# Two diffusion-style transformer blocks on one core: projections and Fourier products moved between attention steps, diagonal products in place of transposes

## The chip, the core and the metric

The kernel runs on one core of a Trainium2 chip. The metric is the device time of one execution in microseconds. Five engines work side by side and meet only at semaphores: TensorE (PE in the profile, its weight loads PEld), VectorE (DVE), ScalarE (ACT), GpSimd (POOL) and SyncE (SP), whose queue issues the weight transfers.

## What is computed

512 tokens of width 1024 pass a first block of two layers and then a second block of one layer, in float32. Only two stages matter here. The first is the mixer of layer 0:

```python
def even_mixer(xn, xcn, w_in, w_out, sink, cos, sin, with_ctx_out):
    proj = xn @ w_in
    f_in = proj[..., :FOURIER_WIDTH]                # 4 heads of 128
    ...
    attn = window_attention(q, k, v, k_c, v_c, sink)
    y = jnp.concatenate([fourier_mix(f_in), attn], axis=-1) @ w_out

def fourier_mix(u):
    uh = u.astype(jnp.float32).reshape(B, N, FOURIER_HEADS, FOURIER_HEAD_DIM)
    y = jnp.fft.fftn(uh, axes=(1, 3), norm='ortho').real
```

The second is the mixer of the second block: a sparse attention of 8 heads (for each query block a compressed, a selected and a window branch, each with its own softmax and gate) beside a stick-breaking attention of 8 heads, whose weights are exp(log_sigmoid(z) + a running sum of log_sigmoid(-z)):

```python
    o_nsa = nsa_mixer(q_n, kc, vc, ksl, vsl, kwn, vwn, gts, positions, ...)
    o_sb = stick_breaking(q_s, k_s, v_s)
    x = x + jnp.concatenate([o_nsa, o_sb], axis=-1) @ w_out[l]
```

## The kernel before, in words

Activations lie transposed in SBUF (features on partitions, 512 tokens along the free side). Every large projection is done as three products on halves: `mm3` (lines 400 to 404) multiplies high by high, high by low and low by high; `act_weights` (L339) casts a block of weights (2048 columns) to its high half, `dve_units` (L351) subtracts to get the low half, and also adds up the modulation's matrix-vector products (L362, L365). The blocks come through two buffers `raw` in the order of `weight_units`. Products of the attentions and of the Fourier mixing are plain float32, which TensorE records as two matmuls each. A transpose is recorded as one.

Each engine's program is written out by hand in one order, with waits on semaphores. The first mixer runs so. `pe_fourier` takes the four Fourier heads c in turn: `pe_over_dims` (L978, 4 products of 256 columns into banks 5 and 6 of PSUM) gives cosine and sine parts, ACT and DVE copy them (L1007, L1024) into `ab`, and 8 products of 512 columns (L998) over the tokens give the head's result, which ACT and DVE split into `xh` and `xl` (L691, L694). Then `pe_first_attention` runs 16 jobs (query block i, pair of heads) as a pipeline of steps: step s has scores(s) (L582, masks L589), turn(s-1) (L649) and attend(s-2) (L684). Beside it DVE takes the maxima (L600, L602), copies half of the turned groups (L675), inverts the sums and multiplies the exponentials by them (`dve_scale`, L636, one instruction for each head), and subtracts (L694); ACT has the exponentials (L611, L614), the other half of the copies (L668) and the casts (L691). Turning a job's weights takes a bank of PSUM for each group of 512 columns; the banks are 4, 5 and 7, and group k waits until group k-3 has been copied.

The second mixer first has its projections (`pe_w_in`): queries of the sparse attention, its keys and values, the compression, then the stick-breaking queries `sq` (4 products of 512 columns, L402 to L404), keys `sk` (4 likewise, scaled into `ksbT` at L1832) and values `sv` (8 token-major products of 256 columns, scaled into `vsb` at L1757). `pe_second_attention` then runs 24 sparse jobs in the same kind of steps, with 4 heads each (for i = 0 to 3 and two key heads: the compressed branch of 31 keys, the selected and the window branch of 128(i+1) keys), and 8 heads of stick-breaking: scores (L1979), ACT's absolute values, exponential and logarithm (L1990 to L1996), DVE's sums (L2006 to L2017), PE's running sums (L2024 to L2027), ACT's exponential (L2038), and attend (L2048). The order of the stick steps on PE is scores(h), sums(h-1), attend(h-2); scores(h+1) waits for ACT's exponential of head h-1. `dve_scale` and `pe_turn` also serve the memory attention (4 jobs) that follows.

## Time and profile before

| What | Value |
|---|---|
| median of 3 runs | 2379.2 us (2374.57 to 2381.82) |
| the profiled execution, its own time | 2376.95 us |
| its span | 2374.9 us |
| TensorE busy (weight loads) | 2217.8 us, 93% (1763.5 us, 74%) |
| VectorE busy | 1099.2 us, 46% |
| ScalarE busy | 774.9 us, 33% |
| mean granted TensorE clock | 0.96 |
| the chain that ended last | PE 83%, DVE 8%, ACT 6% |

The span is that of one profiled execution; its own time adds 2 us around it. The clock is the share of full speed that TensorE was granted.

### The profile page before, as it was taken

Reading aid. Unit: us, or ns where it says so; the run is one execution under the profiler, and the core shown is the slowest. Engines: PE = TensorE matmul, PEld = TensorE weight load, DVE = VectorE, ACT = ScalarE, POOL = GpSimd, SP = SyncE. Lnnn points to the kernel's source line nnn. Section 1 sums busy time; section 2 is a strip of 40 time slices with the busy share of each in tenths; the row PEclk is TensorE's granted clock in tenths of the full one; section 3 lists DMA queues with packets and bytes.
Section 4 is the critical chain, followed back from the end, with each engine's and each line's share of the span. In section 5 each row is a group of like instructions: output and inputs, shape, how many; then the busy total and the mean of one; then the engine's idle time right before and its main releaser. Section 6 shows DMA issues by size and latency. Waiting matters only on the chain.

```text
span 2374.9 us, 25076 instructions
## 1 busy us (share of the span) xinstructions
PE 2217.8 (93%) x10572; PEld 1763.5 (74%) x10572; DVE 1099.2 (46%) x1550; ACT 774.9 (33%) x1149; POOL 87.5 (4%) x84
## 2 busy tenths in 40 slices
PE   6997889999994999999999999899988898999999
PEld 4665678888873888888888888777755576888887
DVE  3637755555528433333534333453474346443421
ACT  4314432222223322222322222323455735222211
POOL 0000000000001000000111100100000001111100
PEclk9999999999996999999999999899887998999999
DMA  7521146555530232323223223223100021323232
GB/s 261 188 88 59 58 133 197 184 195 167 192 103 18 90 106 89 102 98 96 93 92 98 95 98 100 68 90 114 39 1 1 0 72 36 107 89 106 85 98 84
DMA packets 190784, 236.59 MB, mean 100 GB/s; under 512 B 4096, under 2 KB 175392, under 8 KB 190544
## 3 DMA queue, kind: packets, MB, share of 16 engines
q1 hardware_dynamic: 189696, 230.42, 30.1%
q0 software_dynamic: 976, 4.57, 0.6%
q8 instruction: 83, 1.36, 0.2%
q14 instruction: 29, 0.24, 0.0%
HBM read 231.96 MB, written 2.10 MB: 99 GB/s over the span
## 4 chain that ended last, share of the span: by engine, by line
PE 83%; DVE 8%; ACT 6%; issue 2%; DMA 0%; POOL 0%; SPq 0%; DVEq 0%; ACTq 0%; POOLq 0%
PE ps L402 24%; PE ps L403 24%; PE ps L404 24%; ACT pr L611 2%; PE ps L998 1%; PE ps L848 1%; PE ps L468 1%; PE ps L649 1%; DVE pr L636 1%; PE ps L1979 1%; PE ps L582 1%; PE ps L684 1%; DVE wl L351 1%; PE ps L381 1%; DVE sa L1397 1%
## 5 line engine op out<-in xcount | busy, mean ns | idle before, releaser
L402 PE MATMUL ps<-xh,wh 128*128 128x512 f32 x1800 | 714.8, 397 | 48.5 <-DVE xl L694 26.5
L403 PE MATMUL ps<-xl,wh 128*128 128x512 f32 x1800 | 708.1, 393 | 0.0
L404 PE MATMUL ps<-xh,wl 128*128 128x512 f32 x1800 | 707.3, 393 | 0.0
L351 DVE TENSOR_TENSOR wl<-raw,wh 128x2048 fp32r<-128x2048 f32 (+1 forms) x170 | 379.0, 2230 | 493.8 <-ACT wh L339 493.8
L402 PEld LDWEIGHTS ps<-xh,wh 128*128 128x128 f32 x1800 | 341.9, 190 | 128.6 <-issue 25.8
L339 ACT CAST wh<-raw 128x2048 fp32r<-128x2048 f32 (+1 forms) x170 | 314.5, 1850 | 340.7 <-PE ps L404 263.1
L404 PEld LDWEIGHTS ps<-xh,wl 128*128 128x128 f32 x1800 | 341.7, 190 | 73.1
L403 PEld LDWEIGHTS ps<-xl,wh 128*128 128x128 f32 x1800 | 342.1, 190 | 72.0 <-issue 1.2
L402 PE MATMUL ps<-hh,wh 128*128 128x512 f32 x704 | 274.1, 389 | 0.0
L404 PE MATMUL ps<-hh,wl 128*128 128x512 f32 x704 | 273.9, 389 | 0.0
L403 PE MATMUL ps<-hl,wh 128*128 128x512 f32 x704 | 273.9, 389 | 0.0
L1251 ACT CAST hh<-tmp 128x512 fp32r<-128x512 f32 x88 | 54.7, 621 | 330.8 <-DVE tmp L1299 330.8
L404 PEld LDWEIGHTS ps<-hh,wl 128*128 128x128 f32 x704 | 132.2, 188 | 27.4
L402 PEld LDWEIGHTS ps<-hh,wh 128*128 128x128 f32 x704 | 132.2, 188 | 27.4
L403 PEld LDWEIGHTS ps<-hl,wh 128*128 128x128 f32 x704 | 132.2, 188 | 27.4
L1299 DVE TENSOR_TENSOR tmp<-ps,tmp 128x512 f32<-128x512 f32 x88 | 60.8, 691 | 142.4 <-PE ps L404 139.1
L365 DVE SCALAR_TENSOR_TENSOR acc<-raw,sc,acc 128x1024 f32<-128x1024 f32 x70 | 89.8, 1283 | 42.1 <-DMA raw<-in_ada_w 40.6
L611 ACT ACTIVATE pr<-ps,sm 128x512 f32<-128x512 f32 (+5 forms) x144 | 72.7, 513 | 98.5 <-DVE sm L598 58.4
L694 DVE TENSOR_TENSOR hl<-tmp,hh 128x512 fp32r<-128x512 f32 x88 | 61.0, 693 | 60.5 <-ACT hh L1251 60.5
L1320 POOL TENSOR_TENSOR tmp<-tmp,acc 128x512 f32<-128x512 f32 x44 | 56.9, 1295 | 775.2 <-ACT tmp L1233 775.2
L1233 ACT ACTIVATE tmp<-tmp 128x512 f32<-128x512 f32 x44 | 27.8, 632 | 166.3 <-DVE tmp L1266 166.3
L649 PE MATMUL ps<-cst,pr 128*128 128x128 f32 (+1 forms) x368 | 65.7, 326 | 13.8 <-ACT pt L668 6.0
(331 smaller groups left out, 1892.4 us busy)
## 6 DMA issues: line engine op xcount, KB each, us to landing
raw<-in_ffn_w SPq DMA_DIRECT2D x52, 1024.0 KB, 5.4
raw<-in_ada_w SPq DMA_DIRECT2D x42, 1024.0 KB, 5.2
raw<-in_ffn_wg SPq DMA_DIRECT2D x22, 1024.0 KB, 5.4
raw<-in_ffn_wu SPq DMA_DIRECT2D x22, 1024.0 KB, 5.3
raw<-in_ffn_w SPq DMA_DIRECT2D x16, 896.0 KB, 4.6
raw<-in_ffn_wd SPq DMA_DIRECT2D x16, 896.0 KB, 4.7
raw<-in_w_in SPq DMA_DIRECT2D x10, 1024.0 KB, 5.2
raw<-in_ffn_wd SPq DMA_DIRECT2D x8, 1024.0 KB, 5.0
```

The source lines that it names most:

```text
L339: e.copy(wh[k % 2][:, 0:n], raw[i % 2][:, 0:n]).then_inc(*WHI.up(i))
L351: e.tensor_tensor(wl[s][:, 0:n], r[:, 0:n], wh[s][:, 0:n].bitcast(F32), ALU.subtract).then_inc(*WLO.up(i))
L365: e.scalar_tensor_tensor(out=acc[:, :], in0=w, scalar=col, in1=acc[:, :], op0=ALU.mult, op1=ALU.add).then_inc(*VA.up((i, kk), *([i, ("sum" ...
L402: e.matmul(dst, ah, bh, start=start, stop=False)
L403: e.matmul(dst, ah, bl, start=False, stop=False)
L404: return e.matmul(dst, al, bh, start=False, stop=stop)
L611: e.activation(prs[J.name][:, J.par, g, 0:J.width], ps[:, o:o + J.width], ACT.Exp, bias=m, accum_out=sm[:, J.par, 4 + g:5 + g]).then_inc(* ...
L649: m = e.transpose(bank[0:w, o:o + P], prs[J.name][:, J.par, g, col:col + w], ident)
L694: e.tensor_tensor(dst, src, high.bitcast(F32), ALU.subtract).then_inc(*VX.up(*keys))
L1251: e.copy(hidden[f][0][:, i, :], tmp[i % 2][:, :]).then_inc(*AX.up((f, i)))
L1299: e.tensor_tensor(t, pb[2 + cc], t, ALU.mult).then_inc(*VF.up(("up", f, i)))
L1320: e.tensor_tensor(t, t, rsx, ALU.mult).then_inc(*GP.up(("gate", f, i)))
```

## The change

It has five parts; some helpers moved by a few lines, so that L636, L649, L998 and L2038 of the kernel before are L632, L650, L994 and L2042 in the changed one.

1. The stick-breaking keys and values leave the projections and are done by `pe_stick_in` in 16 pieces, one in each of the first 16 steps of the sparse attention, between scores(s) and turn(s-1), in bank 7: 8 pieces of values, then 8 half products of keys. The weight blocks change places accordingly (`sv` before `sk`); four blocks are prepared (cast and subtraction) in steps 1, 5 and 9 for these and in 18 and 20 for the output projection.
2. Of the Fourier mixing, head 0 stays; the 24 products over tokens of heads 1 to 3 are done two at a time in steps 0 to 11 of the first attention, in bank 7. `ab` gets four buffers, `over_dims` four banks. Three more modulation units (13, 14, 15) are added up between the attention's steps.
3. The softmax's scaling goes into the turn: instead of multiplying each head's exponentials, DVE makes a diagonal matrix of the inverse sums for all heads of a job in one instruction, and PE multiplies by it instead of transposing.
4. The turns have banks 4 and 5 alone, so group k waits for the copy of group k-2.
5. ACT loads one table set, `natural_log_exp_and_others`, ahead of the stick-breaking heads. The sparse outputs of query blocks 0 and 1 are first copied to `tmp` and split into `xh` and `xl` in steps 17 and 19, since the pieces still read those.

```diff
+            eye = ident.unsqueeze(1).broadcast_to([P, nh, P])
+            e.tensor_tensor(diagonal(J), eye, rs.unsqueeze(2).broadcast_to([P, nh, P]), ALU.mult).then_inc(
+                *VS.up((J.name, "diagonal", J.n)))
-            for g in range(nh):
-                p = prs[J.name][:, J.par, g, 0:J.width]
-                e.tensor_scalar(p, p, rs[:, g:g + 1], None, ALU.mult).then_inc(*VS.up((J.name, "scaled", J.n, g)))
...
-                        m = e.transpose(bank[0:w, o:o + P], prs[J.name][:, J.par, g, col:col + w], ident)
+                        m = e.matmul(bank[0:w, o:o + P], prs[J.name][:, J.par, g, col:col + w], diagonal(J)[:, g],
+                                     start=True, stop=True, skip_group_check=True)
...
+        def pe_over_tokens(e, c, tb):
+            if c and tb == 0:
+                e.wait_ge(*VX["mix", c - 1])
+            e.wait_ge(*dims_copied(c, tb))
+            for z, tab in ((0, "cn"), (1, "sn")):
+                m = e.matmul(pb[7], ab[c][:, tb, z * P:(z + 1) * P], b1(tab, T, tb * T), start=tb == 0 and z == 0,
+                             stop=tb == 3 and z == 1)
...
+            for c in range(1, 4):
+                pe_over_dims(e, c)
+            for tb in range(4):
+                pe_over_tokens(e, 0, tb)
+            e.wait_ge(*dims_copied(3, 2))
+            pe_modulation(e, 0, 2, pb[0])
...
             for s in range(n + 2):
                 if s < n:
                     pe_scores(e, first_[s])
+                if s < 12:
+                    c, tb = 1 + s // 4, s % 4
+                    pe_over_tokens(e, c, tb)
+                if s == 12:
+                    e.wait_ge(*VX["mix", 3])
+                    pe_modulation(e, 0, 3)
                 if 0 < s <= n:
-                    pe_turn(e, first_[s - 1])
+                    pe_turn(e, first_[s - 1], (4, 5))
...
+                if s in (1, 4, 6, 8, 12):
+                    dve_units(e, {1: 13, 4: 14, 6: 15, 8: 16, 12: 17}[s])
...
+        def pe_stick_in(e, p):
+
+            if p < 8:
+                y, tb = p // 4, p % 4
+                u = of["sv", y]
+                if tb == 0:
+                    e.wait_ge(*WLO[u])
+                if p:
+                    e.wait_ge(*AE["sv", ((p - 1) // 4, (p - 1) % 4)])
+                pe_proj_tok(e, 7, u, 0, 256, xh, xl, tb).then_inc(*MM.up(("sv", y, tb), *([("w", u)] if tb == 3 else [])))
+                return
+            c, half = (p - 8) // 2, p % 2
...
+            for k in range(4 * half, 4 * half + 4):
+                m = mm3(e, pb[7], hi[:, k, cols], lo[:, k, cols], xh[:, k, :], xl[:, k, :], k == 0, k == NC - 1)
...
+        steps = {1: ("sv", 1), 5: ("sk", 0), 9: ("sk", 1), 18: ("out2", 0), 20: ("out2", 1)}
...
                 elif s < NN + 8:
                     pe_stick_scores(e, s - NN)
+                if s < 16:
+                    pe_stick_in(e, s)
                 if 0 < s <= NN:
-                    pe_turn(e, nsa_[s - 1])
+                    pe_turn(e, nsa_[s - 1], (4, 5))
...
                 elif s < NN + 8:
+                    if s == NN:
+                        e.preload_act_table_set("natural_log_exp_and_others")
                     act_stick_logs(e, s - NN)
...
+                if s in steps:
+                    act_weights(e, of[steps[s]])
...
+                if 8 < s < 16 and s % 2:
+                    dve_stick_in(e, "sk", (s - 9) // 2)
+                if s in steps:
+                    dve_units(e, of[steps[s]])
```

TensorE from the Fourier stage to the first scores (`fT` is the Fourier input, `ab` its parts, `b1c` the tables, `acc` the modulation's sums). Before:

```order
L978 MATMUL ps<-b1c,fab 128x256 x4
L967 MATMUL ps<-cst,tmp 128x128 x6
L978 MATMUL ps<-b1c,fab 128x256 x4
L998 MATMUL ps<-b1c,fab 128x512 x8
L978 MATMUL ps<-b1c,fab 128x256 x4
L381 MATMUL ps<-cst,acc 128x1 x8
L998 MATMUL ps<-b1c,pr 128x512 x8
L978 MATMUL ps<-b1c,fab 128x256 x4
L998 MATMUL ps<-b1c,fab 128x512 x8
L998 MATMUL ps<-b1c,pr 128x512 x8
L582 MATMUL ps<-kT,qT 128x128
```

and now:

```order
L986 MATMUL ps<-b1c,fT 128x256 x4
L968 MATMUL ps<-cst,tmp 128x128 x6
L986 MATMUL ps<-b1c,fT 128x256 x12
L994 MATMUL ps<-b1c,ab 128x512 x8
L379 MATMUL ps<-cst,acc 128x1 x8
L580 MATMUL ps<-kT,qT 128x128
...
L587 MATMUL ps<-bcs 128x128 x2
L994 MATMUL ps<-b1c,ab 128x512 x2
```

Of the 32 products over tokens, 8 stay ahead of the attention, and two follow each of twelve scores.

ScalarE over one stick-breaking head in the steady state (`C2S` holds the logarithms, `pt` the weights). Before:

```order
L1990 ACTIVATE C2S<-ps 128x512
L1992 ACTIVATE C2S<-ps 128x768
L1994 ACTIVATE C2S<-C2S 128x1280
L1996 ACT_TABLE_LOAD
L1996 ACTIVATE C2S<-C2S,cst 128x1280
L2038 ACT_TABLE_LOAD
L2038 ACTIVATE pt<-ps 128x512
L2038 ACTIVATE pt<-ps 128x768
L691 CAST xh<-ps 64x512
```

and now:

```order
L1994 ACTIVATE C2S<-ps 128x512
L1996 ACTIVATE C2S<-ps 128x768
L1998 ACTIVATE C2S<-C2S 128x1280
L2000 ACTIVATE C2S<-C2S,cst 128x1280
L2042 ACTIVATE pt<-ps 128x512
L2042 ACTIVATE pt<-ps 128x768
L692 CAST xh<-ps 64x512
```

Of 16 table loads in this stage one is left, ahead of the first head.

## Rows read from the trace of the kernel before

**Rows 1.** Windows by stage: Fourier, first attention, stick keys and values, sparse, stick.

```profile
core 0: us, PE busy (x) PEld busy (x) DVE busy (x) ACT busy (x) POOL busy (x), PEclk, DMA share, GB/s
144.14:187.54 43.40, 40.00 (x121) 20.80 (x119) 15.55 (x21) 7.96 (x16) 0.00 (x0) 0.96 0.29 96
187.54:279.65 92.11, 68.31 (x720) 53.57 (x720) 75.29 (x184) 48.34 (x148) 0.00 (x0) 0.93 0.11 36
1643.02:1689.64 46.62, 45.31 (x290) 41.19 (x289) 11.94 (x8) 11.70 (x14) 0.00 (x0) 1.00 0.29 91
1689.64:1801.65 112.01, 97.89 (x720) 64.27 (x721) 82.23 (x274) 60.92 (x229) 0.00 (x0) 0.84 0.00 1
1801.65:1902.18 100.53, 86.65 (x323) 51.66 (x321) 35.40 (x89) 70.07 (x77) 0.00 (x0) 0.88 0.00 0
```

**Rows 2.** Timeline of PE in the Fourier stage: start, duration, line, tiles, count, [idle before].

```profile
144.14 2.25 PE L978 MATMUL ps<-b1c,fab 128*128 128x256 f32 x8
...
149.22 7.03 PE L998 MATMUL ps<-b1c,fab 128*128 128x512 f32 x16
156.09 1.03 PE L978 MATMUL ps<-b1c,fab 128*128 128x256 f32 x4
...
158.95 1.96 PE L381 MATMUL ps<-cst,acc 128*128 128x1 f32 x16
```

**Rows 3.** Timeline of PE, one step of the first attention.

```profile
218.48 0.37 PE L582 MATMUL ps<-kTs,qT 64*128 64x128 f32 x1 [1.29 <-ACT pr L611]
...
220.02 1.29 PE L649 MATMUL ps<-cst,pr 128*128 128x128 f32 x10
...
223.63 0.37 PE L582 MATMUL ps<-kTs,qT 64*128 64x128 f32 x1 [1.07 <-ACT pr L611]
```

**Rows 4.** Timeline of DVE, the same step.

```profile
219.04 1.02 DVE L636 TENSOR_SCALAR pr<-pr,sm 128x640 f32<-128x640 f32 x2
...
220.60 0.82 DVE L600 TENSOR_REDUCE sm<-ps 128x1 f32<-128x640 f32 x1
```

**Rows 5.** Timeline of PE: four plain float32 products of 128 columns.

```profile
1962.02 1.05 PE L468 MATMUL ps<-cst,hs 128*128 128x128 f32 x8
```

**Rows 6.** Timeline of PE, turns of the sparse attention.

```profile
1743.04 1.54 PE L649 MATMUL ps<-cst,pr 128*128 128x128 f32 x12
...
1748.29 3.08 PE L649 MATMUL ps<-cst,pr 128*128 128x128 f32 x12 [0.59 <-DVE pr L636]
...
1780.43 0.66 PE L649 MATMUL ps<-cst,pr 128*128 128x128 f32 x4 [2.51 <-DVE pt L675]
```

**Rows 7.** Groups by line: busy, mean ns, idle before; first whole span, then the sparse stage.

```profile
L351 DVE TENSOR_TENSOR wl<-raw,wh 128x2048 fp32r<-128x2048 f32 (+1 forms) x170 | 379.0, 2230 | 493.8 <-ACT wh L339 493.8
L339 ACT CAST wh<-raw 128x2048 fp32r<-128x2048 f32 (+1 forms) x170 | 314.5, 1850 | 340.7 <-PE ps L404 263.1
...
L365 DVE SCALAR_TENSOR_TENSOR acc<-raw,sc,acc 128x1024 f32<-128x1024 f32 x70 | 89.8, 1283 | 42.1 <-DMA raw<-in_ada_w 40.6
...
L636 DVE TENSOR_SCALAR pr<-pr,sm 128x31 f32<-128x31 f32 (+4 forms) x92 | 24.1, 326 | 0.8
```

**Rows 8.** Timeline of ACT, one stick-breaking head.

```profile
1873.22 1.27 ACT L1994 ACTIVATE C2S<-C2S 128x1280 f32<-128x1280 f32 x1
1874.51 1.28 ACT L1996 ACT_TABLE_LOAD   x1
1875.80 1.36 ACT L1996 ACTIVATE C2S<-C2S,cst 128x1280 f32<-128x1280 f32 x1
1877.18 1.28 ACT L2038 ACT_TABLE_LOAD   x1
```

**Rows 9.** Timeline of PE, the same head.

```profile
1869.92 2.42 PE L1979 MATMUL ps<-qsT,ksbT 64*128 64x512 f32 x8 [1.24 <-ACT pt L2038]
...
1876.22 2.38 PE L2048 MATMUL ps<-pt,vsb 128*128 128x512 f32 x8
1879.83 2.42 PE L1979 MATMUL ps<-qsT,ksbT 64*128 64x512 f32 x8 [1.24 <-ACT pt L2038]
```

More of the change, by code:

```diff
@@ L222, in program @@
         part.close()
+        first.close()
         part = ExitStack()
+        pt = sb("pt", [P, 2, 1280], F32, part)
+        ab = [sb(f"ab{c}", [P, 4, 256], F32, part) for c in range(4)]
         b1c = sb("b1c", [P, NB1C], F32, part)
-        fab = sb("fab", [P, 3072], F32, part)
-        fT = fab[:, 0:2048].rearrange("p (c t) -> p c t", c=4)
+        fT = sb("fT", [P, 4, T], F32, part)
         qT = sb("qT", [P, 4, T], F32, part)
@@ L266, in program @@
         hid = sb("hid", [P, 2, 2 * NCMP], F32, second)
+        rcol = sb("rcol", [P, 4], F32, second)
+        rsm = ssum
         part = ExitStack()
@@ L1011, in act_fourier @@
             act_values(e, "v", pb[2], T, vt)
[L1012 to L1017 removed]
+            act_values(e, "vc", pb[3], LC, vct)
+            for c in range(1, 4):
+                act_over_dims(e, c)
+            act_fourier_put(e, 0)
         def dve_over_dims(e, c):
@@ L1665, in pe_w_in @@
[L1665 to L1676 removed]
+            for y in range(2):
+                u = of["sq", y]
+                e.wait_ge(*WLO[u])
+                for cc in range(2):
+                    c = 2 * y + cc
+                    e.wait_ge(*(VE["scaled", "gates"], AE["kc"], VE["sq", 0], VE["sq", 1])[c])
+                    pe_proj(e, cc, u, cc * P, xh, xl).then_inc(*MM.up(("in2", "sq", c), *([("w", u)] if cc else [])))
+                    if c == 0:
+                        pe_rope2(e, "kw", "ks", kwT[:, 0, :])
+                        for b in range(4):
+                            m = e.transpose(pb[2][:, b * 24:(b + 1) * 24], tmp[1][0:24, b * P:(b + 1) * P], cst[0:24, 0:24])
+                        m.then_inc(*ST.up(("turned", "gates")))
+                        pe_head_sums(e, "kc", "kw", 0, n)
+                    elif c == 1:
+                        pe_head(e, "kc", None, 3, 0, n)
+                    elif c == 2:
+                        pe_cmp_turn(e, 1)
+                        for j in range(2):
+                            pe_rope2(e, ("kc", j), ("kc", 0) if j else "kw", kcC[:, j * NCMP:(j + 1) * NCMP], NCMP, "kc")
+                if y == 0:
+                    pe_cmp(e, 1, 1)
+                else:
+                    e.wait_ge(*AE["hid", 1])
+                    e.wait_ge(*VE["sq", 3])
+                    for j in range(2):
+                        for f in range(2):
+                            m = e.matmul(pb[1][0:NCMP, j * P:(j + 1) * P], hid[:, f, j * NCMP:(j + 1) * NCMP],
+                                         w2c[:, 1, f, :], start=f == 0, stop=f == 1)
+                    m.then_inc(*MM.up(("in2", "vc")))
@@ L1971, in pe_stick_scores @@
                 e.wait_ge(*EX["nsa", NN - 1, 3])
+                e.wait_ge(*VE["sk", 3])
             elif h == 1:
@@ L2095, in act_second_attention @@
                             r, cs, cols, src = nsa_places(J, o)
-                            act_put(e, xh[r, cs, cols], src, ("nsa", J.n, o))
+                            if J.i > 1:
+                                act_put(e, xh[r, cs, cols], src, ("nsa", J.n, o))
+                            else:
+                                e.copy(nsa_early(J.i)[r, cs], src).then_inc(*AE.up(("nsa", J.n, o)))
+                    if s in (17, 19):
+                        i = (s - 17) // 2
+                        e.wait_ge(*AE["nsa", 6 * i + 5, 1])
+                        act_put(e, xh[:, 0:4, i * P:(i + 1) * P], nsa_early(i), ("early", i))
                 elif s > 1:
```

216 lines of the change are left out of this document (75 added, 141 removed).

## The prediction

> **What bounds the kernel now.** I read the page first: TensorE is busy 93% of the span and carries 83% of the chain, so a stage gets shorter either where TensorE has less to do or where it now waits. Then I cut the two mixers into stages with the windows [rows 1]. Nearly all of the change lies in five of them, from 144.14 to 279.65 us (Fourier stage and first attention) and from 1643.02 to 1902.18 us (stick keys and values, sparse attention, stick-breaking). In the Fourier stage PE is busy 40.0 of 43.4 us, and with the keys and values 45.3 of 46.6: there the work itself sets the time. In the three attention stages it is not so plain: PE is busy 68.3 of 92.1 us at a granted clock of 0.93, 97.9 of 112.0 at 0.84 and 86.7 of 100.5 at 0.88. A busy figure taken at half clock is inflated, so I multiply: at full clock (2.4 GHz) the work is about 68.3 x 0.93 = 64, 97.9 x 0.84 = 82 and 86.7 x 0.88 = 76 us. The room that work from elsewhere can fill is the rest, 28, 30 and 24 us. What ends PE's waits there is to be seen in single steps. In the first attention scores(s+1) waits 1.1 to 1.3 us for ACT's exponentials [rows 3], and those wait for DVE, which goes round once in 5.15 us, 1.02 of it in the two scalings and 0.82 in one maximum [rows 4]. In the stick stage ACT is the pacemaker: one head takes 9.91 us, PE is idle for 1.24 of it until ACT's last exponential [rows 9], and between ACT's instructions stand two table loads of 1.28 us [rows 8].
>
> **Price of a turn.** The trace has no product with a diagonal, but plain float32 products of the same 128 columns: four of them, eight records, last 1.05 us [rows 5]. A burst's last record has a tail of 0.16 us that does not hold up what follows (16 records last 7.03 us and the next begins after 6.87 [rows 2]), so one product costs (1.05 - 0.16) / 4 = 0.22 us. A transpose costs 1.54 / 12 = 0.13, or 0.12 without the tail [rows 6]. Each of the 368 turned blocks thus costs TensorE 0.10 us more: 144 in the first attention, +14; 192 in the sparse one, +19; 32 in the memory attention, +3. As bounds I take 0.05 and 0.14 (the tail left in). The Trainium skill speaks against this part: its page TensorE: Matmul & The Clock Gate (Terms) says that transpose mode makes FP32 four times faster. By that a product would cost 0.50 us and the 336 blocks of the two mixers would add over 120 us; rows 5 and 6 give a factor of 1.8, and I go by them. For DVE the scaling becomes one instruction of 256 or 512 columns. I take 0.42 and 0.69 us, by proportion from the 0.82 us that DVE takes over 640 columns and what it pays per instruction; a fused 0.27 is the low end, 1.02, that is no gain, the high one [rows 4]. That frees DVE of some 0.6 us a step, 9 in the first attention and 8 of the 24 us in the sparse one [rows 7].
>
> **First mixer.** Eight products over tokens take 6.87 us [rows 2], 0.86 each. Now 24 of the 32 leave the Fourier stage. What stays is: 16 products over dimensions at 0.43 (two of them, four records, take 1.03 less the tail; the eight of 144.14, with a wait in them, 2.25) 7, six transposes 1, 8 products over tokens 7, the modulation 2, waits for copies 1.5 [rows 2]. That is 18.5 us in place of 43.4: **-25**. In the attention they come back. A step at 640 columns had 5.15 - 1.07 = 4.1 us of PE work [rows 3]; it gets 1.72 (two products) and ten turned blocks at 0.10, and is 6.8 us long. DVE's round is then about 4.5 us, hidden in it. The whole stage: 64 + 20.6 + 14 = 99 us of PE work at full clock, and PE no longer waits in the first twelve steps except some 0.5 us in every second one, where the third group waits for its bank (two banks in place of three). The last steps keep the waits that they had. Three added modulation units are 6 x 1.28 us of DVE [rows 7], hidden as long as PE's step is 2 us longer than DVE's round; uncovered they would cost 8. I take 101 us in place of 92.1: **+9**, between +5 and +16. Net **-16**.
>
> **Keys and values.** The 46.6 us of PE work go from before the sparse attention into its steps: -46.6 there. The attention then has 82 + 46.6 + 19 = 148 us of PE work, in 16 steps of some 6.2 us and 8 of some 5.5. With that much work between scores(s) and scores(s+1), DVE and ACT (82 and 61 us busy in all) are always ahead in the first 16 steps, so TensorE should stay at full clock there, where it had 0.84 [rows 1]. What is not hidden: the blocks of weights prepared in steps 1, 5 and 9 (cast 1.85 after the copies on ACT, subtraction 2.23 on DVE [rows 7]) delay the next maxima by about 1 us beyond PE's step, 3 in all; those of steps 18 and 20, where no piece gives cover, by 1 to 3 each, 4 in all. And from step 16 on a turn of three or four groups on two banks waits for copies that stand behind the maxima and exponentials of the next job; with three banks such a wait took 2.51 us [rows 6]. It comes earlier now and is partly repaid by the shorter scaling: +1 on each of four turns, 4. Sum 148 + 11 = 159, against 46.6 + 112.0 = 158.6: **0**. Half clock in the last eight steps would add to it, a better fit would take from it: -10 to +15. This is the step that I am least sure of.
>
> **Stick-breaking.** 15 of 16 table loads go, 19.2 us of ACT [rows 8]. But per head only PE's wait can be saved, 1.24 of the 9.91 us: PE has 8.67 us of work per head [rows 9], and ACT's round without the loads (9.91 - 2.57 = 7.34) is below it. Over eight heads 10 us. The rest of the gain is at the ends, where nothing overlaps: the first head, during which PE waits for the turns' copies behind the logarithm, and the last head's chain through logarithm, sums and exponential, three loads or 4 us; and the stretches at half clock, which followed from waits. I take 84 us in place of 100.5: **-16**, between -10 (the waits alone) and -24 (all loads and full clock). The Trainium skill's ScalarE: Activation LUTs (What ACT_TABLE_LOAD costs) adds a drain of 1.38 us to each load. By it a head would save 5.3 us of ACT's time; the logarithm starts 0.01 us after the load's end and the load 0.02 after the exponential's [rows 8], so there is no such drain here, and PE's work caps the gain in either case.
>
> **The rest.** Memory attention: eight turned blocks a step on PE +0.8, DVE's scaling -0.45, four steps: +1 (-2 to +3). The early copies and late splits of the sparse outputs cost nothing: ACT has 51 us idle in that stage [rows 1]; without that cover 1 us each. Sum -16 + 0 - 16 + 1 = -31 against the profiled execution's 2376.95: **2346 us**. The median of the runs shown is 2.2 us above that execution, so I say 2347.
>
> **Rivals.** (a) *The moved work is hidden whole.* Then the first mixer saves 25, the keys and values 46.6 and the stick stage 20: 2377 - 91 = 2286. Against it: TensorE's room at full clock in the two receiving stages is 28 and 30 us, and the turns alone take 14 and 19 of it. Chance 0.03. (b) *The stick stage gains little*, since TensorE sets its pace and remains at half clock at its ends: -6 in place of -16, and the sparse stage loses 5: 2361. Chance 0.15. (c) *Slower: the sparse steps become a chain of turn, copy, turn on two banks, at half clock.* Place: steps 12 to 24. Price: at half clock the twelve transposes took 3.08 in place of 1.54 us [rows 6]. If the clock of the sparse stage stays at the old 0.84, 148 us of work take 148 / 0.84 = 176, and with the 11 of waits 187: +28; with the bank waits at 2.5 us in each of the eight long turns another 12, and the first attention at 0.93 +7. That gives 2346 + 47 = 2393. It decides from a clock of about 0.87 in the sparse stage with such waits. For it: half clock came in this stage whenever PE waited. Against: the pieces fill just these waits. Chance 0.06. (d) *Better fit:* TensorE at full clock throughout and almost no waits in the sparse stage, -9 there, -18 first mixer, -20 stick: 2331. Chance 0.2. (e) That the moved work stands where it is hidden from nobody (a piece waits for its weight block, a transfer being late) would show as waits of PE on the subtraction; the blocks have landed long before (the DMA share is 0.00 in the sparse stage [rows 1]), 0.02, at some 2370.
>
> **How the numbers follow.** My forecast, 2347, has 0.54. The range 2329 to 2366 takes in (b) and (d), leaves out (a), (c), (e) and the ends of my own terms where several coincide. A measurement of this kernel can tell some 0.3%, 7 us, from no change. Faster by more needs under 2372: my case, (a), (b), (d), 0.90 after the tails; within it 0.05; slower 0.05.
>
> **What the changed profile would show.** Right: the Fourier stage under 21 us, the first attention near 101 with a clock near 1; the sparse stage from the last `sq` product to the first stick scores near 159 us with waits of PE for ACT and DVE only behind the prepared blocks and from step 16 on; L650 at 0.22 us a block; one table load in the stick stage, heads 8.7 us apart there, with no wait on L2042. Wrong: a turned block at 0.4 us or more at full clock; steps without pieces as long as those with; stick heads still 9.9 us apart.

## The result, and the profile after

The changed kernel took **2365.8 us** (median of six, 2360.3 to 2370.4), the kernel before beside it 2378.2 (2374.6 to 2381.8): a ratio of 0.9948, 95% interval 0.9931 to 0.9965. It is faster, by 12.4 us where 31 were forecast: 0.5%, with the interval clear of 1. The time lies 19 us above the forecast of 2347, just under the range's upper end of 2366. The execution that was profiled is the slowest of the six, 2370.41 us, 6.5 us less than the profiled one of before. All stage figures below are from profiled executions.

First the windows by stage of the changed kernel, with the columns of [rows 1]: Fourier stage, first attention, sparse attention with the keys and values in it, stick-breaking.

```profile
144.84:161.58 16.74, 16.28 (x73) 11.51 (x71) 6.73 (x12) 6.62 (x13) 0.00 (x0) 1.00 0.19 63
161.58:280.22 118.64, 105.58 (x912) 80.49 (x912) 76.90 (x177) 51.42 (x150) 0.00 (x0) 0.94 0.16 54
1643.40:1809.63 166.23, 156.59 (x1186) 125.67 (x1184) 85.95 (x206) 76.82 (x246) 0.00 (x0) 0.94 0.10 33
1809.63:1896.50 86.87, 80.21 (x340) 50.12 (x339) 35.01 (x88) 49.67 (x61) 0.00 (x0) 0.96 0.00 1
```

| stage | before [rows 1] | after | difference | forecast |
|---|---|---|---|---|
| Fourier | 43.4 | 16.7 | -26.7 | -25 |
| first attention | 92.1 | 118.6 | **+26.5** | +9 |
| keys, values and sparse attention | 158.6 | 166.2 | **+7.6** | 0 |
| stick-breaking (up to the next projection) | 100.5 | 86.4 | -14.1 | -16 |
| sum | | | -6.7 | -32 |

The two profiled executions differ by 6.5 us, so nothing is left for the rest of the kernel. (The next projection begins at 1895.99; the last window runs half a microsecond on.) The two receiving stages took back more than the Fourier stage gave, and the gain that remains is the stick-breaking's. The places to look at are the 17.5 us too much in the first attention and the 7.6 in the sparse one.

**One step of the first attention that goes wrong.** The timeline of PE in the changed kernel, two steps, a normal one and a long one. L994 is the piece over tokens, L650 the turn by diagonals, L685 the product with the values.

```profile
201.44 1.94 PE L994 MATMUL ps<-b1c,ab 128*128 128x512 f32 x4
203.22 2.55 PE L650 MATMUL ps<-tmp,pr 128*128 128x128 f32 x20
205.70 0.88 PE L685 MATMUL ps<-pt,vt 128*64 128x128 f32 x12
...
208.48 1.94 PE L994 MATMUL ps<-b1c,ab 128*128 128x512 f32 x4
210.25 1.95 PE L650 MATMUL ps<-tmp,pr 128*128 128x128 f32 x16
214.31 1.22 PE L650 MATMUL ps<-tmp,pr 128*128 128x128 f32 x4 [2.11 <-ACT pt L669]
215.46 1.55 PE L685 MATMUL ps<-pt,vt 128*64 128x128 f32 x12
...
219.33 1.94 PE L994 MATMUL ps<-b1c,ab 128*128 128x512 f32 x4
```

From piece to piece it is 7.04 us in the first and 10.85 in the second. In the second PE does eight of its ten turned blocks and then stands for 2.11 us before the third group, which needs the bank of the first group back: ACT's copy (L669) has not come. What follows the wait is at half clock besides: four records take 1.22 us, and twelve of L685 1.55, where twelve took 0.88 a step before. The same stretch on DVE and on ACT shows why the copy is late. L363 is the modulation unit, L598 the maxima, L600 their scaling, L609 the exponentials.

```profile
207.35 0.61 DVE L695 TENSOR_TENSOR xl<-ps,xh 64x128 fp32r<-64x128 f32 x2 [0.39 <-ACT xh L692]
207.99 2.60 DVE L363 SCALAR_TENSOR_TENSOR acc<-raw,sc,acc 128x1024 f32<-128x1024 f32 x2
210.62 0.82 DVE L598 TENSOR_REDUCE sm<-ps 128x1 f32<-128x640 f32 x1
```

```profile
211.73 0.80 ACT L609 ACTIVATE pr<-ps,sm 128x640 f32<-128x640 f32 x1 [4.13 <-DVE sm L600]
...
213.68 0.57 ACT L669 COPY pt<-ps 128x512 f32<-128x512 f32 x1
```

The scores have left PE by 208.5 (the piece behind them begins at 208.48). DVE is in a unit of 2.60 us until 210.59, so the maximum begins 2 us late; ACT idles 4.13 us for it, and only behind its two exponentials, at 213.68, does it copy the bank that PE was done with at about 211.3. The three longest steps (10.59, 10.85 and 9.25 us from piece to piece, beginning at 190.85, 208.48 and 226.36) are just those behind the units of steps 4, 6 and 8. The unit of step 1 makes no long step: the turns near it have eight blocks, two groups for two banks, and no third group that waits.

**Sparse attention.** The timeline of PE in its late steps, where no piece is left.

```profile
1776.58 2.00 PE L650 MATMUL ps<-tmp,pr 128*128 128x128 f32 x16
1781.50 3.44 PE L650 MATMUL ps<-tmp,pr 128*128 128x128 f32 x16 [2.92 <-DVE pt L676]
...
1786.34 2.03 PE L650 MATMUL ps<-tmp,pr 128*128 128x128 f32 x16
1790.72 3.31 PE L650 MATMUL ps<-tmp,pr 128*128 128x128 f32 x16 [2.35 <-DVE pt L676]
```

Four groups on two banks: two groups, a wait of 2.9 or 2.4 us for a copy, two more groups, and these at half clock (16 records 3.4 us in place of 2.0).

**Stick-breaking.** One head on ACT after, against [rows 8]: no load is left between exponential (L1998), logarithm (L2000) and the last exponential (L2042), and ACT now has idle time before it.

```profile
1854.10 1.27 ACT L1998 ACTIVATE C2S<-C2S 128x1280 f32<-128x1280 f32 x1
1855.40 1.36 ACT L2000 ACTIVATE C2S<-C2S,cst 128x1280 f32<-128x1280 f32 x1
1857.30 1.30 ACT L2042 ACTIVATE pt<-ps 128x512 f32<-128x512 f32 x2 [0.53 <-PE ps L2031]
```

PE goes from head to head without a wait, 1850.80 and 1859.40 in the next rows, 8.60 us against 9.91 in [rows 9].

```profile
1850.80 2.42 PE L1983 MATMUL ps<-qsT,ksbT 64*128 64x512 f32 x8
...
1859.40 2.42 PE L1983 MATMUL ps<-qsT,ksbT 64*128 64x512 f32 x8
```

### The profile page after: what moved, and what is told of

Its sections match the earlier page's. It is cut to its first block, busy times and chain, and to the rows that moved or that the text cites. A ratio compares the mean times of both kernels' runs of the same rounds, so it can differ in the third digit from the quotient of the medians.

```text
span 2368.6 us, 25694 instructions
## 1 busy us (share of the span) xinstructions
PE 2238.4 (95%) x10940; PEld 1801.6 (76%) x10940; DVE 1079.3 (46%) x1444; ACT 759.4 (32%) x1136; POOL 87.6 (4%) x84
## 4 chain that ended last, share of the span: by engine, by line
PE 87%; DVE 7%; ACT 4%; issue 1%; DMA 0%; SPq 0%; DVEq 0%; ACTq 0%
PE ps L400 24%; PE ps L402 24%; PE ps L401 24%; PE ps L650 3%; PE ps L580 2%; PE ps L685 2%; PE ps L849 1%; PE ps L466 1%; ACT pr L609 1%; PE ps L994 1%; DVE wl L349 1%; ACT wh L337 1%; PE ps L1983 1%; PE ps L2028 1%; PE ps L379 1%
## 5 line engine op out<-in xcount | busy, mean ns | idle before, releaser
L402 PEld LDWEIGHTS ps<-hh,wl 128*128 128x128 f32 x704 | 132.2, 188 | 27.5
L400 PEld LDWEIGHTS ps<-hh,wh 128*128 128x128 f32 x704 | 132.2, 188 | 27.4
L401 PEld LDWEIGHTS ps<-hl,wh 128*128 128x128 f32 x704 | 132.2, 188 | 27.3
L650 PE MATMUL ps<-tmp,pr 128*128 128x128 f32 (+1 forms) x736 | 99.8, 289 | 20.0 <-ACT pt L669 10.3
L650 PEld LDWEIGHTS ps<-tmp,pr 128*128 128x128 f32 (+1 forms) x736 | 92.4, 195 | 31.9 <-ACT pt L669 11.7
L363 DVE SCALAR_TENSOR_TENSOR acc<-raw,sc,acc 128x1024 f32<-128x1024 f32 x70 | 89.8, 1283 | 43.5 <-DMA raw<-in_ada_w 41.9
L609 ACT ACTIVATE pr<-ps,sm 128x512 f32<-128x512 f32 (+5 forms) x144 | 72.7, 514 | 96.8 <-DVE sm L596 51.2
```

The costliest lines, as they stand in the source:

```text
L363: e.scalar_tensor_tensor(out=acc[:, :], in0=w, scalar=col, in1=acc[:, :], op0=ALU.mult, op1=ALU.add).then_inc(*VA.up((i, kk), *([i, ("sum" ...
L400: e.matmul(dst, ah, bh, start=start, stop=False)
L401: e.matmul(dst, ah, bl, start=False, stop=False)
L402: return e.matmul(dst, al, bh, start=False, stop=stop)
L609: e.activation(prs[J.name][:, J.par, g, 0:J.width], ps[:, o:o + J.width], ACT.Exp, bias=m, accum_out=sm[:, J.par, 4 + g:5 + g]).then_inc(* ...
L650: m = e.matmul(bank[0:w, o:o + P], prs[J.name][:, J.par, g, col:col + w], diagonal(J)[:, g], start=True, stop=True, skip_group_check=True)
```

## The experiments

Each was timed in five rounds against the kernel before on the same chip. The ratios are to that kernel, whose median was 2376 to 2378 us in every batch, so they can be set beside the change's own 0.9948; differences between medians of two batches can be off by those 2 us. The theory: modulation units that clump on DVE, copies that stand behind exponentials on ACT, and two banks instead of three, together make PE wait; not the work that was moved. The rival: TensorE's added work sets both stages.

### First four: units, pieces, rows, table

**e1, units spread.** One of a unit's two instructions at the end of a step, where two stood together.

```diff
-                if s in (1, 4, 6, 8, 12):
-                    dve_units(e, {1: 13, 4: 14, 6: 15, 8: 16, 12: 17}[s])
+                halves_ = {1: (13, 0), 2: (13, 1), 3: (14, 0), 4: (14, 1), 5: (15, 0), 6: (15, 1), 7: (16, 0), 8: (16, 1), 12: (17, 0), 13: (17, 1)}
+                if s in halves_:
+                    dve_half_unit(e, *halves_[s])
```

> The changed kernel, with each modulation unit of the first attention (two DVE instructions of 1.30 us in a row at the end of steps 1, 4, 6, 8, 12) dealt out one instruction a step, at the ends of steps 1 to 8, 12 and 13. Theory T (the units in DVE's order delay the maxima, the exponentials and so the copy of the first turned bank, and TensorE stands before the third bank): the three long steps of 10.6, 10.85 and 9.25 us fall to about 7.1 to 7.6, the attention goes from 118.6 to 109 to 112 us, the run from 2366 to 2357 to 2360. Rival R (TensorE's added work and its clock set the stage): the attention stays within 2 us of 118.6 and the run at 2364 to 2367.

Measured: **2355.7 us, 0.9914 (0.9900 to 0.9929)**. The attention took 110.48 us, in the window of that run:

```profile
162.33:272.81 110.48, 102.48 (x913) 78.27 (x913) 76.93 (x177) 51.03 (x150) 0.00 (x0) 0.97 0.18 58
```

8.2 us less, with the same number of products and DVE instructions. PE is idle 8.0 in place of 13.1 us and busy 3.1 less. Its work at full clock is 102.48 x 0.97 = 99.4 us, the changed kernel's (105.58 x 0.94 = 99.2) within the rounding of the clock, so the 3.1 are half clock.

The idle part is the sure one. Two runs below have the changed kernel's first attention untouched: it took 116.43 us in e11 and 119.63 in e5. PE was idle in them for 13.9 and 13.4 us, as in the changed kernel, but busy for 102.5 and 106.3.

```profile
161.69:278.12 116.43, 102.50 (x913) 78.84 (x913) 76.93 (x177) 51.37 (x150) 0.00 (x0) 0.97 0.17 55
```

With e9, which repeats this run's edit (110.77 us, 8.8 idle), spreading the units takes 4 to 6 us off the idle time in every pair. How much half clock stands behind the waits differs by up to 3.8 us between executions of the same code, and e11 has no more of it than e1. The step that took 10.85 us now takes 7.94. PE, the same two pieces and what lies between:

```profile
206.55 1.94 PE L1012 MATMUL ps<-b1c,ab 128*128 128x512 f32 x4
208.33 1.95 PE L668 MATMUL ps<-tmp,pr 128*128 128x128 f32 x16
211.06 0.71 PE L668 MATMUL ps<-tmp,pr 128*128 128x128 f32 x4 [0.79 <-ACT pt L687]
...
214.49 1.94 PE L1012 MATMUL ps<-b1c,ab 128*128 128x512 f32 x4
```

The wait is 0.79 us, not 2.11, and what follows is at full clock. So the clump is one cause, worth 6 to 9 us of the stage and 8 to 10 of the whole time (by ratio and by median); the expected "about 7.1 to 7.6" for the long steps was a little too good.

**e2, all Fourier pieces ahead**, the pieces of each quarter in banks 7 and 4 in turn.

```diff
-            for tb in range(4):
-                pe_over_tokens(e, 0, tb)
-            e.wait_ge(*dims_copied(3, 2))
-            pe_modulation(e, 0, 2, pb[0])
+            for c in range(4):
+                for tb in range(4):
+                    pe_over_tokens(e, c, tb)
+                if c == 0:
+                    e.wait_ge(*dims_copied(3, 2))
+                    pe_modulation(e, 0, 2, pb[0])
...
-                if s < 12:
-                    c, tb = 1 + s // 4, s % 4
-                    pe_over_tokens(e, c, tb)
```

> The changed kernel, with all sixteen Fourier pieces over tokens done before the first attention (two banks in turn), the units, the two turn banks and the diagonals as in the changed kernel. The Fourier stage grows by 12 pieces of 1.73 us, from 16.7 to 37 to 40 us. Theory T (the long steps come from DVE's order, not from the pieces): they stay long, the attention falls by the pieces' 20.6 us alone, to 98, and the run is within 3 us of 2366. Rival A (the pieces fill time in which TensorE would wait): the attention falls only to 102 to 108, the run rises to 2370 to 2376. Rival B (the pieces are what pushes the steps over): the attention falls to 90 to 94 and the run to 2358 to 2362.

Measured: **2380.7 us, 1.0018 (1.0009 to 1.0027)**: rival A, and past its upper end. Its Fourier stage and its attention:

```profile
144.91:181.82 36.91, 36.91 (x120) 20.44 (x119) 8.11 (x14) 6.51 (x14) 0.00 (x0) 1.00 0.09 29
181.82:295.94 114.12, 87.14 (x866) 73.50 (x865) 75.32 (x175) 51.18 (x149) 0.00 (x0) 0.93 0.17 56
```

That was the most telling run. With 20 us of pieces taken out of it, the attention is only 4.5 us shorter than the changed kernel's 118.6 (2.3 than e11's), and 22 us longer than the 92.1 of before. Here my theory was wrong too: it had taken the waits for fixed. PE waited 13.7 us for ACT's copies, against 6.3 with the pieces. So the pieces do hide waits, some 16 us of them (20.6 less 4.5), but for the most part waits that the change itself had made: with three banks, in e8, 16.7 us of the stage go.

**e3, rows scaled and transposed again** in all three attentions, the rest as changed.

```diff
-            eye = ident.unsqueeze(1).broadcast_to([P, nh, P])
-            e.tensor_tensor(diagonal(J), eye, rs.unsqueeze(2).broadcast_to([P, nh, P]), ALU.mult).then_inc(
-                *VS.up((J.name, "diagonal", J.n)))
+            for g in range(nh):
+                p = prs[J.name][:, J.par, g, 0:J.width]
+                e.tensor_scalar(p, p, rs[:, g:g + 1], None, ALU.mult).then_inc(*VS.up((J.name, "scaled", J.n, g)))
```

> The changed kernel, with the rows scaled by DVE and turned by transposes again in all three attentions, the rest as changed. Theory T: TensorE has 0.1 us less for each turned block, DVE 0.7 to 1.3 us more a step, in front of units and maxima: the long steps grow to 11 to 12 us, the others shorten by at most 1 us, and the run is at 2363 to 2370. Rival R (TensorE's added work sets the stage): the attention falls by most of the 14 us that the products by the diagonals add there, to 105 to 108, and the run to 2350 to 2356.

Measured: **2352.1 us, 0.9900 (0.9884 to 0.9915)**, 14 us under the changed kernel. The number is the rival's, the place is not: the first attention fell by 3.1 us only, the sparse part from 166.2 to 151.0.

```profile
160.24:275.78 115.54, 94.43 (x769) 66.14 (x769) 85.17 (x193) 50.62 (x150) 0.00 (x0) 0.90 0.17 56
1639.27:1790.23 150.96, 134.68 (x1010) 100.56 (x1008) 93.86 (x277) 77.11 (x246) 0.00 (x0) 0.94 0.11 36
```

In the first attention the theory comes nearer: the long steps stay at 11.05, 10.65 and 10.69 us from piece to piece, the normal ones fall from 7.0 to 6.3, and PE's waits for ACT's copies grow from 6.3 to 11.0 us. In the sparse one PE is busy 22 us less (156.6 to 134.7), and 15 of them come off the stage (against e11's 162.0 it is 11): there TensorE's work is what counts. The first attention has modulation units in its steps and the sparse one none; that this is the reason for the difference was not tested.

**e4, the kernel before with the table load alone.**

```diff
                 elif s < NN + 8:
+                    if s == NN:
+                        e.preload_act_table_set("natural_log_exp_and_others")
                     act_stick_logs(e, s - NN)
```

> The kernel before, with one load of the table that holds both Exp and Ln ahead of the stick heads and nothing else. If the changed kernel's gain in the stick stage (100.5 to 86.4 us) is this load alone, the heads stand 8.5 to 8.7 us apart, the stage falls by 10 to 13 us and the run is at 2365 to 2368, as fast as the whole change. If the gain came from the smaller DVE and PE work around it, the heads stay 9.5 us or more apart and the run is at 2373 to 2378.

Measured: **2362.2 us, 0.9940 (0.9927 to 0.9954)**, 14.0 us faster with this one line, 3 us beyond the expected range. It is as fast as the whole change. The heads stand 8.60 us apart, and the stick stage fell by 16.0 us:

```profile
1800.93:1885.48 84.55, 80.04 (x323) 48.85 (x321) 35.57 (x89) 49.87 (x61) 0.00 (x0) 0.93 0.00 1
```

### Four more: banks, and the diagonals by themselves

**e5, the third bank back in the sparse attention from job 16 on** (the last key piece has then left bank 7).

```diff
+        switch = nsa_[16].k0
+
+        def late_banks(k, before_=False):
+            def at_(k):
+                return (4, 5)[k % 2] if k < switch else (7, 4, 5)[(k - switch) % 3]
...
-                    pe_turn(e, nsa_[s - 1], (4, 5))
+                    pe_turn(e, nsa_[s - 1], late_banks)
```

> The changed kernel, with bank 7 given back to the sparse attention's turned blocks as soon as the last key piece has left it (from job 16 on, three banks in turn). Its PE rows there show waits of 0.88, 2.92, 2.35 and 0.98 us for a copy out of one of two banks. Theory B (two banks cost the late steps): they go, the sparse steps end 4 to 7 us earlier, the run is at 2359 to 2362. Rival (the same steps wait next for their maxima or for the weight units behind steps 18 and 20): at most 1.5 us, 2364 to 2366.

Measured: **2356.4 us, 0.9919 (0.9907 to 0.9931)**, 9.4 us under the changed kernel, more than theory B gave. The same turns as above, now PE's L655:

```profile
1776.82 1.82 PE L655 MATMUL ps<-tmp,pr 128*128 128x128 f32 x8 [2.02 <-DVE pt L682]
...
1781.01 5.22 PE L655 MATMUL ps<-tmp,pr 128*128 128x128 f32 x32
```

Four groups (32 records) follow each other without a wait. The part up to the stick scores took 157.5 us, and the stick stage gained too: PE waits 2.4 us in it for the last copies in place of 4.4, and its granted clock is 1.00 in place of 0.96. e9, with the same edit, has the same two stages within 0.02 us (157.54 and 81.36).

```profile
1643.07:1800.59 157.52, 153.06 (x1186) 122.50 (x1184) 85.96 (x206) 76.95 (x246) 0.00 (x0) 0.96 0.11 35
1800.59:1881.95 81.36, 76.76 (x338) 48.06 (x337) 34.94 (x88) 49.20 (x61) 0.00 (x0) 1.00 0.00 1
```

**e6, e1 and e3 together.**

> The changed kernel with both edits of the first four runs that gained: modulation units one instruction a step, and rows scaled by DVE with transposes. If the two prices are independent (10 us and 14 us below the changed kernel): 2340 to 2344. If DVE, which with the rows is 8 us busier in the first attention, has no room left for a spread unit, the halves give only 3 to 6 us: 2346 to 2350.

Measured: **2346.9 us, 0.9881 (0.9865 to 0.9898)**, inside the second case: from e3, spread units gave 5 us, not 10. With rows PE waits 7.4 us for ACT's copies again, against 2.6 with diagonals: DVE has less room for the half unit.

**e7, the kernel before with the diagonals alone** (the edit of e3 the other way round, on three banks).

> The kernel before, with the diagonal products alone in all three attentions, on its three banks. If their price is TensorE's time whatever stands around them, the first attention goes from 92 to 100 us or more, the sparse attention from 112 to about 125, the run to 2388 to 2396. If their price needs the two banks and the pieces of the changed kernel, both stages grow by at most 3 us and the run is at 2374 to 2382.

Measured: **2375.3 us, 0.9989 (0.9978 to 0.9999)**. They cost nothing there: the attention took 91.98 us and the sparse attention 112.07, within 0.2 us what they take in [rows 1].

```profile
188.86:280.84 91.98, 81.96 (x865) 70.67 (x865) 67.76 (x168) 48.79 (x148) 0.00 (x0) 0.94 0.11 36
1691.15:1803.22 112.07, 108.72 (x896) 80.90 (x897) 74.59 (x203) 61.57 (x229) 0.00 (x0) 0.92 0.01 1
```

PE is 13.7 and 10.8 us busier, all of it in time in which it had waited. Once the pieces stand between the steps, the same exchange costs 9 to 14 us (e1 to e6 8.8, e9 to e10 9.7, change to e3 13.7).

**e8, e2 with three banks in the first attention.** Modulation 3's products go behind the last turned block of step 12.

```diff
-                if s == 12:
-                    e.wait_ge(*VX["mix", 3])
-                    pe_modulation(e, 0, 3)
...
-                    pe_turn(e, first_[s - 1], (4, 5))
+                    pe_turn(e, first_[s - 1])
...
+                if s == 12:
+                    J = first_[s - 1]
+                    k = max(k for k, _ in score_groups(J) if k % 3 == 2)
+                    e.wait_ge(*turned(J, k))
+                    pe_modulation(e, 0, 3)
```

> The run with all Fourier pieces ahead of the attention (2380.7 us, attention 114.1, long steps 10.9, 10.7, 10.7), with three banks for the turned blocks of the first attention. Theory (a late exponential costs through the copy of the bank that the third group waits for): the long steps fall to 8 to 9, the attention to 104 to 108, the run to 2371 to 2375. Rival (the late maxima delay the step by themselves, whatever the banks): the attention stays at 111 or more and the run at 2377 to 2381.

Measured: **2366.3 us, 0.9952 (0.9936 to 0.9968)**, 14.4 us under e2. The attention fell by 16.7 us, more than I had expected.

```profile
182.29:279.66 97.37, 82.12 (x866) 70.22 (x865) 75.16 (x175) 50.13 (x149) 0.00 (x0) 0.95 0.20 66
```

The waits of PE in that stage, first in e2 with two banks, then in e8 with three (us in total, times, longest):

```profile
PE ps L650 <- ACT pt L669: 13.7, 4, 4.3
PE ps L580 <- ACT pr L609: 9.3, 5, 3.7
PE ps L650 <- DVE pt L676: 2.4, 3, 0.8
```

```profile
PE ps L580 <- ACT pr L609: 13.7, 8, 3.7
```

With three banks all waits for copies are gone, and those for exponentials (L609) grow a little. The units clump in both.

### Combinations, and whether the pieces pay

**e9, e1 and e5 together; e10, e1, e3 and e5 together.**

> The changed kernel with its own diagonals, with the modulation units one instruction a step and the third bank given back from sparse job 16 on. The two gains lie in different stages (10 us and 10 us alone): if they add, 2344 to 2348. If one takes the other's time away (later waits, another stretch at half clock), 2350 or more.

> As the run before it, with rows scaled by DVE and transposes in place of the diagonals. With the pieces beside them both stages are near TensorE's own time, so the 0.1 us for each turned block should still count: 2335 to 2341. If with three late banks and spread units TensorE has slack again, as it had in the kernel before, where the diagonals cost nothing: 2342 to 2347.

Measured: e9 **2348.9 us, 0.9873 (0.9856 to 0.9890)**, a little short of full addition; e10 **2339.2 us, 0.9836 (0.9815 to 0.9857)**, 9.7 us under it and 39 under the kernel before: the fastest version of the study. The rows won in both stages (110.8 to 107.1 us and 157.5 to 150.8).

**e11, the changed kernel without its table load** (the diff of e4, taken out).

> The changed kernel without its one load of the table that holds Exp and Ln. If the load is all that the change gains (it took 14 us off the kernel before, alone), this run is as slow as the kernel before: 2377 to 2381. If half of the stick stage's gain comes from the rest of the change: 2370 to 2374.

Measured: **2377.7 us, 1.0002 (0.9989 to 1.0016)**. Its stick stage took 99.1 us and ACT shows the loads again:

```profile
1862.36 1.27 ACT L1998 ACTIVATE C2S<-C2S 128x1280 f32<-128x1280 f32 x1
1863.65 1.28 ACT L2000 ACT_TABLE_LOAD   x1
1864.94 1.36 ACT L2000 ACTIVATE C2S<-C2S,cst 128x1280 f32<-128x1280 f32 x1
```

Together with e4 this closes the account: one load is all that the change gains. Its three large parts come to nothing together, within the 4 us that the interval leaves.

**e12 to e15, Fourier pieces ahead with spread units:** e13 is e8 with e1's edit, e14 that with rows, e12 that with the late bank too, e15 is e12 again. In these four the products of modulation 3 stand before the last turned block of step 12, which writes over their bank, so that modulation is not the reference's; the work is the same.

> As the run with rows, halves and the late bank, but with all Fourier pieces ahead of the first attention, which then has three banks. With clumped units and diagonals the Fourier stage and the attention took 134.3 us this way and 135.4 as changed. If moving the pieces is worth what hides beside them once units no longer clump, this run is 3 to 8 us slower than the one with the pieces between the steps: 2341 to 2348. If three banks give as much as the moved pieces, it is within 2 us of it.

> The changed kernel with all Fourier pieces ahead of the first attention, three banks there, and the modulation units one instruction a step. Against the run with spread units and the pieces between the steps (16.7 and 110.5 us of the two stages, 2355.7 in all). If the move pays by what hides beside it, this one has 36.9 us and 95 to 98, 5 to 8 us more in the first mixer: 2361 to 2364. If the third bank gives back as much as the move, 36.9 and 88 to 91: 2354 to 2358.

> The same with rows scaled by DVE and transposes, against the run with rows and spread units (16.7 and 109.1, 2346.9 in all). If the move pays, 36.9 and 96 to 99, 2353 to 2358; if not, 2345 to 2348.

> The run with all Fourier pieces ahead, rows, spread units and the late third bank, once more: 2345 to 2352 if its first measurement (2349.6) holds.

Measured: e12 2349.6 us (0.9881, 0.9863 to 0.9900), e15 2348.9 (0.9882, 0.9868 to 0.9895), e13 2363.1 (0.9941, 0.9928 to 0.9953), e14 2355.7 (0.9916, 0.9903 to 0.9930). All four are on the side of "the move pays"; e12 lies 1.6 us above even the range that it had given for that, so the move was worth some 10 us there and not 3 to 8.

**e16 and e17: e13 and e12 with those products behind the block**, as in e8.

> The changed kernel with all Fourier pieces ahead of the first attention, three banks there, the modulation units one instruction a step, and the products of modulation 3 at the end of step 12. If the move pays by what hides beside it once units are spread: 36.9 us and 95 to 98 for the two stages (16.7 and 110.5 with the pieces between the steps), 2360 to 2364 in all. If not: 2354 to 2358.

> The same with rows scaled by DVE, transposes, and the late third bank, against the run with the pieces between the steps (16.7 and 107.1, 2339.2 in all). If the move pays: 2346 to 2351. If not: 2337 to 2341.

Measured: e16 **2361.4 us, 0.9933 (0.9919 to 0.9948)**; e17 **2351.0 us, 0.9879 (0.9859 to 0.9899)**. The first attention of e16 and of e17:

```profile
182.46:278.53 96.07, 81.86 (x866) 70.10 (x865) 75.17 (x175) 49.98 (x149) 0.00 (x0) 0.95 0.21 67
```

```profile
181.63:280.14 98.51, 69.75 (x722) 55.07 (x721) 83.01 (x191) 49.71 (x149) 0.00 (x0) 0.90 0.20 65
```

**The first mixer, all runs** (Fourier stage plus first attention, us):

| pieces, banks | clumped units | spread units |
|---|---|---|
| before (rows, three banks, two units in the steps) | 135.5 | |
| the same with diagonals | e7 135.4 | |
| ahead, two banks, diagonals | e2 151.0 | |
| ahead, three banks, diagonals | e8 134.3 | e16 133.0, e13 132.2 |
| between the steps, two banks, diagonals | change 135.4, e11 133.2, e5 136.4 | e1 127.2, e9 127.5 |
| ahead, three banks, rows | | e17 135.4 |
| between the steps, two banks, rows | e3 132.3 | e6 125.8, e10 123.9 |

Each figure is one profiled execution, and the same code differs by up to 3 us (change, e11, e5). Read down the first column: giving up the bank costs 16.7 us, moving the pieces gives back 15.6 (14.6 to 17.8 with e5 and e11). Read down the second: with spread units the move with its lost bank gains 5.8 us with diagonals (e16 to e1: 5.7 us of the whole time) and 11.5 with rows (e17 to e10: 11.8). Spreading the units gains 8.2 with two banks and the pieces between the steps, 1.3 with three banks and the pieces ahead, which is no more than executions differ. Bank and place of the pieces change together in these two figures; two banks with the pieces ahead and spread units was not run. The waits speak for the bank: a third one takes all of PE's waits for copies away with the units still in clumps (e2 to e8), and spread units take 6.3 us of them down to 2.6 with two banks (e1). So the units and the lost bank are in the main one price, not two: a third bank lets PE finish its turn while an exponential is late, two do not.

## Why the prediction was right or wrong

- **Price of a turn: right.** Eight products took 1.95 us and ten 2.55, which is 0.22 and 0.24 each without the tail of 0.16; DVE's diagonal is 0.42 us at 256 columns, the value taken, and 0.69 at 512. The Trainium skill's factor of four (TensorE: Matmul & The Clock Gate, Terms), 0.50 us by my estimate from it, is not seen here: against the 0.12 us of a transpose the factor is 1.8 to 2.
- **Fourier stage, -25: right** (-26.7; the waits for copies that I had allowed for did not come).
- **First attention, +9: wrong, +26.5, and this is the step that failed.** The work was right: 99 us at full clock forecast, 99.2 measured. What failed is the sentence that "PE no longer waits in the first twelve steps except some 0.5 us in every second one", and the one that the three added units are "hidden as long as PE's step is 2 us longer than DVE's round; uncovered they would cost 8". They were not hidden: a unit is 2.60 us in one piece, DVE's order puts it ahead of the next maxima, and a mean slack of 2.3 us a step (6.8 less 4.5) does not cover 2.60 at once. I counted DVE's time where its order decides. That e1 gains 8.2 us in this stage, so near my 8, is luck: my 8 was the time of six DVE instructions, and what was measured is PE's idle time and half clock behind five units, 6 to 9 us by the executions of the same code. In the sum, the 17.5 us too much are 11 us of idle time (13.1 where I had 2) and 6.4 of half clock (105.6 less 99.2), which I had put at nothing by taking 99 us of work as 99 us of time. I priced the bank at 0.5 us; a late exponential makes it 2.11 and half clock behind it (e2 against e8: 16.7 for the whole stage without pieces). Last, my sum had 2 us for all waits though I had written that "the last steps keep the waits that they had"; in e1, 3.7 of the 8.0 us of idle time are one wait for an exponential at the end. The range for this term, +5 to +16, did not hold it; e1 would be +18.4, so the clump alone does not bring the stage back to the forecast either.
- **Keys and values, 0: too good, by 7.6 us in the profiled run.** The work was right again: 148 forecast, 156.59 x 0.94 = 147.2. The same code took 162.0 and 160.4 us in e11 and e16, 163.2 and 163.5 in e1 and e8, 160.3 in e2, so some 4 us of the 7.6 belong to this one execution; it is the slowest of six. What stays is the bank again, "+1 on each of four turns, 4": with the third bank given back 157.5, 4.4 us less than the mean of those five, and 5 more in the stick stage (86.4 to 81.4), which I had not connected with it at all. With rows in place of diagonals the stick stage keeps its 86.4 us in spite of the third bank (e10); why is open. Keys and values were the step that I had named as the least sure.
- **Stick-breaking, -16: right in size and cause.** -14.1; e4 has -16.0 in this stage and -14.0 us of the whole time by the load alone, e11 +11.9 by taking it out. The head is 8.60 us apart (8.67 forecast) and no drain beyond the loads' 1.28 us appears, as said ahead of the result.
- **Memory attention and the rest, +1: near enough.** From its first scores to the projection behind it the memory attention took 22.7 us before and 22.8 after (1975.70 to 1998.37, 1969.22 to 1991.98), and the four stages sum to -6.7 of -6.5.
- **The sum:** the last step has a slip. The median before is 2.2 us above the profiled execution, and 2346 + 2.2 is 2348, not 2347; it changes nothing in the account.
- **The rivals.** (c) had a right mechanism, turn, copy, turn on two banks at half clock, but put it in the sparse stage alone, where it needed a clock of 0.87 and found 0.94, and gave it the whole stage in place of a few late steps. (b) comes nearest to the number, with 2361, for the wrong reason: it had the stick stage gain 6 us, and it gained 14. None of them put the bank and the units together in the first attention.
- **What I did not ask:** whether each part pays. The 33 us of added TensorE work stood in the sum, and the 17 us of DVE time that they bought was nowhere on the path. e3 shows 14 us to be had by not making that exchange.

Not tried: a third bank beside the pieces in the first attention (scores take four, turns two, attention and pieces one each: all eight are in use); ACT's copy of the first group put ahead of its exponentials; and the keys and values back in front of the sparse attention with everything else as changed, so their own worth is known only as 158.6 to 150.8 us with rows (before to e10).

## What to carry to other kernels

When filler work is moved between the steps of a pipeline, sum not only the bottleneck engine's work but walk the order of each helper engine through one step: the longest single instruction run in front of the next step's first instruction must fit into that step's gap, not its mean slack. Buffers given up for the filler are part of its price, and it can be as large as all that the filler hides; measure filler and buffers apart (here 15.6 and 16.7 us in the first mixer). Exchanging work from a helper to the bottleneck engine is free only as long as that engine waits; once filler comes in, the exchange must be looked at again, and a one-line edit in a bundle should be timed alone.

## What the runs showed that I had not expected

- Removing a wait gained more than the wait. PE's waits for copies of turned blocks, from the late sparse steps to the second stick head, sum to 11.6 us in the changed kernel and to 4.4 in e5, 7.2 less. The same edit takes 10.6 us off the two stages between e1 and e9 (249.5 to 238.9); the granted clock of the stick stage, whose heads were not edited, went from 0.96 to 1.00 in both.
- The same code at the same work had PE busy for 102.5, 105.6 and 106.3 us in three executions of the first attention, with idle times of 13.9, 13.1 and 13.4 us: what half clock adds behind the same waits differs from execution to execution, so a gain in busy time needs more than one pair of profiles.
- More TensorE work at the same end. e7 added 24.5 us of PE busy time to two stages and neither grew by more than 0.1 us; the sparse one's granted clock rose from 0.84 [rows 1] to 0.92 at the same length.
- ACT's table load costs its 1.28 us and nothing beside it: in e11 the logarithm starts 0.01 us behind its end.
